# Every fourth gated row of the first placing round made on ScalarE instead of VectorE

## What is computed

```python
def _peer(h, wq, subkeys, u, v):
    q = (hf @ wq).reshape(n, PEER_HEADS, 2, PEER_QUERY_DIM // 2)
    s = jnp.einsum('nhpd,hpkd->nhpk', q, subkeys).astype(jnp.float32)
    sv, si = lax.top_k(s, PEER_TOPK)
    cand = (sv[:, :, 0, :, None] + sv[:, :, 1, None, :]).reshape(n, PEER_HEADS, PEER_TOPK * PEER_TOPK)
    cand_idx = (si[:, :, 0, :, None] * PEER_N_KEYS + si[:, :, 1, None, :]).reshape(n, PEER_HEADS, PEER_TOPK * PEER_TOPK)
    top_v, top_pos = lax.top_k(cand, PEER_TOPK)
    experts = jnp.take_along_axis(cand_idx, top_pos, axis=-1)
    gates = jax.nn.softmax(top_v, axis=-1).astype(h.dtype)
...
        act = jax.nn.gelu(jnp.einsum('td,tkd->tk', xb, u[eb]), approximate=False)
        return jnp.einsum('tk,tkd->td', gb * act, v[eb])
```

## Time and profile before

| what | value |
|---|---|
| median of 3 runs | 3841.91 us (3835.98 to 3842.95) |
| the profiled execution | 3840.35 us, span 3838.6 us |
| TensorE matmul busy | 3649.0 us (95%) |
| VectorE busy | 2594.1 us (68%) |
| GpSimd busy | 1618.4 us (42%) |
| ScalarE busy | 695.1 us (18%) |

### The profile page before, as it was taken

How to read it: one execution, slowest core, us unless ns; L and a number is a source line. 1 busy time by engine, 2 the same in 40 slices (tenths; PEclk the granted TensorE clock), 3 DMA queues, 4 the chain that set the end, 5 groups by cost and what they waited for, 6 DMA issues and landing times. The chain is left out here.

```text
span 3838.6 us, 39934 instructions
## 1 busy us (share of the span) xinstructions
PE 3649.0 (95%) x13726; PEld 2080.8 (54%) x13726; DVE 2594.1 (68%) x5994; ACT 695.1 (18%) x1579; POOL 1618.4 (42%) x1498
## 2 busy tenths in 40 slices
PE   5888899999999999999989898999999999999997
PEld 3455676555555555554455567765555555555543
DVE  7784999957666667676624749987776565565444
ACT  1242366200000000000013525661000000000000
POOL 0200255456566544454402005454777564444330
PEclk9999999999999999999999999999999999999999
DMA  7323145789999999999830122557999999899774
GB/s 271 108 79 121 39 132 154 265 332 391 380 373 374 376 378 373 379 372 359 354 125 2 63 110 78 158 154 280 409 410 410 379 349 365 341 358 361 286 298 156
DMA packets 365049, 1026.96 MB, mean 268 GB/s; under 512 B 30352, under 2 KB 132016, under 8 KB 364208
## 3 DMA queue, kind: packets, MB, share of 16 engines
q0 software_dynamic: 147456, 536.94, 36.5%
q1 hardware_dynamic: 118352, 436.07, 29.7%
q10 hardware_dynamic: 99040, 51.40, 4.8%
HBM read 965.07 MB, written 59.22 MB: 267 GB/s over the span
## 5 line engine op out<-in xcount | busy, mean ns | idle before, releaser
L1881 PE MATMUL ps<-colsT,arena 128*128 128x384 f32 x4096 | 1361.6, 487 | 7.0 <-DMA arena<-in_peer_ut 4.8
L1881 PEld LDWEIGHTS ps<-colsT,arena 128*128 128x128 f32 x4096 | 776.3, 190 | 588.2 <-issue 100.2
L1915 PE MATMUL ps<-arena 128*128 128x512 f32 x1536 | 676.5, 592 | 0.0
L1390 POOL DMA_INDIRECT proj<-in_peer_u,eidx x336 | 475.8, 1416 | 230.8 <-DVE modbc L1582 113.4
L1390 POOL DMA_INDIRECT proj<-in_peer_v,eidx x335 | 360.3, 1075 | 315.7 <-DVE colsT L1593 216.5
L1915 PEld LDWEIGHTS ps<-arena 128*128 128x128 f32 x1536 | 291.8, 190 | 345.2 <-issue 317.6
L1582 DVE CUSTOM_DVE_ANT_0 proj<-proj,rows 128x1024 f32<-128x1024 f32 x336 | 399.4, 1223 | 57.4 <-DMA proj<-in_peer_u,eidx 55.7
L1376 POOL TENSOR_SCALAR x<-iota,modbc 128x128 f32<-128x128 f32 x192 | 144.7, 770 | 680.9 <-ACT modbc L1710 554.9
L1593 DVE SCALAR_TENSOR_TENSOR colsT<-proj,modbc,colsT 128x1024 f32<-128x1024 f32 x330 | 409.7, 1286 | 12.6 <-DMA proj<-in_peer_v,eidx 12.5
L1915 PE MATMUL ps<-arena,x 128*128 128x512 f32 x768 | 337.7, 592 | 0.0
L1915 PE MATMUL ps<-arena,rows 128*128 128x512 f32 x768 | 337.7, 592 | 0.0
(11 more groups left out here) (294 smaller groups left out, 3719.1 us busy)
## 6 DMA issues: line engine op xcount, KB each, us to landing
arena<-in_peer_ut SPq DMA_DIRECT2D x256, 512.0 KB, 6.8
arena<-in_peer_v SPq DMA_DIRECT2D x256, 512.0 KB, 6.7
gmat_d<-arena ACTq DMA_DIRECT2D x24, 2048.0 KB, 9.3
arena<-gmat_d SPq DMA_DIRECT2D x64, 768.0 KB, 9.0
proj<-in_w_adaT SPq DMA_DIRECT2D x51, 512.0 KB, 9.1
modbc<-in_w_adaT SPq DMA_DIRECT2D x19, 512.0 KB, 8.9
rows<-in_w_adaT SPq DMA_DIRECT2D x18, 512.0 KB, 3.5
arena<-in_w_in SPq DMA_DIRECT2D x2, 4224.0 KB, 16.4
```

The source lines that it names most:

```text
L1390: pool.indirect_dma_start(ring[slots[at]], None, tab, bass.IndirectOffsetOnAxis(ap=eidx[:, b * SLOTS + q:b * SLOTS + q + 1], axis=0)).then ...
L1881: mm = pe.matmul(ps[:, 2 + j % 2, 0:ND], utab[:, j % UR, k], hT[:, k, NG:T], start=(k == 0), stop=(k == KT - 1))
L1915: mm = pe.matmul(ps[:, Y_BANKS[2 * d + c2], :], wT[j % CR][:, d * P:(d + 1) * P], vtab[:, j % VR, c2 * 512:(c2 + 1) * 512], start=(j == 0) ...
```

## The change

In round one (groups below 32 of each layer) VectorE leaves out the fourth token of each group, and ScalarE makes that row in two instructions: |j - column| by Abs with scale -1 and the index as bias, then Relu with the negated gate as scale and the gate as bias, which is the gate at distance zero and at most zero, so clipped, elsewhere. The negated gates come from one more copy in `turned_out` (region `ngT`). ScalarE makes these rows for the first four groups in one batch after the first marks, and later two at a time after the marks of a pair. TensorE waits for a new semaphore, `b_act`, besides `b_made`, whose count now goes by three a group in round one (`dve_rows`). Rounds two and three are untouched.

```diff
+        ngT = region(modbc, 2 * D + 7 * P, P)
...
+        def act_row(n):
+            return n < P // 4
...
+                        if t % 4 == 3 and act_row(n // 4):
+                            continue
                         dve.tensor_scalar(bring[:, n % B_TOK], iota128[:, :], ijgT[:, d % 2, 1, t:t + 1],
...
-                    c.link(act.activation(ijgT[:, d % 2, 0], ps[:, 0, 0:P], ACT.Copy, scale=-1.0))
+                    c.done(act.activation(ijgT[:, d % 2, 0], ps[:, 0, 0:P], ACT.Copy, scale=-1.0))
+                    if d == 0:
+                        c.done(act.activation(ngT, ps[:, 0, 2 * P:3 * P], ACT.Copy, scale=-1.0))
+                    c.wait()
...
+                def gated_rows(groups):
+                    groups = [n for n in groups if act_row(n)]
+                    if not groups:
+                        return
+                    if groups[0] < A_GRP:
+                        act.wait_ge(tr_out, 1)
+                    else:
+                        act.wait_ge(g_mm, groups[-1] - A_GRP + 1)
+                    for n in groups:
+                        t = 4 * n + 3
+                        c.done(act.activation(bring[:, t % B_TOK], iota128[:, :], ACT.Abs, scale=-1.0, bias=ijgT[:, 0, 1, t:t + 1]))
+                    c.wait()
+                    for n in groups:
+                        t = 4 * n + 3
+                        act.activation(bring[:, t % B_TOK], bring[:, t % B_TOK], ACT.Relu, scale=ngT[:, t:t + 1],
+                                       bias=ijgT[:, 0, 2, t:t + 1]).then_inc(b_act, 1)
...
+                        if pair + A_GRP < P // 4:
+                            gated_rows([d * (P // 4) + pair + A_GRP + h for h in range(2)])
...
                     for q in range(A_GRP):
                         mark_rows((k - 1) * (P // 4) + q)
+                    gated_rows([(k - 1) * (P // 4) + q for q in range(A_GRP)])
...
-                        pe.wait_ge(b_made, 4 * n + 4)
+                        pe.wait_ge(b_made, dve_rows(n))
+                        if act_row(n):
+                            pe.wait_ge(b_act, n + 1)
```

More of the change, by code:

```diff
@@ L198, in build @@
     sc_half = sem("sc_half")
+    b_act = sem("b_act")
     dots_ready, gelu_ready, coef_ready = sem("dots_ready"), sem("gelu_ready"), sem("coef_ready")
@@ L1274, in act_marks, with dve_rows @@
             return n % 2 == 0
+        def act_row(n):
+            return n < P // 4
+        def dve_rows(n):
+            return 4 * (n + 1) - min(n + 1, P // 4)
         def sc_row(r):
@@ L1706, in turned_out @@
                     if d >= 2:
-                        act.wait_ge(b_made, (d - 1) * P)
+                        act.wait_ge(b_made, dve_rows((d - 1) * (P // 4) - 1))
                         act.wait_ge(p_made, (d - 1) * (P // 2))
-                    c.link(act.activation(ijgT[:, d % 2, 0], ps[:, 0, 0:P], ACT.Copy, scale=-1.0))
+                    c.done(act.activation(ijgT[:, d % 2, 0], ps[:, 0, 0:P], ACT.Copy, scale=-1.0))
+                    if d == 0:
+                        c.done(act.activation(ngT, ps[:, 0, 2 * P:3 * P], ACT.Copy, scale=-1.0))
+                    c.wait()
                     act.activation(ijgT[:, d % 2, 1:3].rearrange("p a t -> p (a t)"), ps[:, 0, P:3 * P], ACT.Copy).then_inc(tr_out, 1)
```

## The result

| | before | changed |
|---|---|---|
| median | 3839.36 us (4 runs, 3835.98 to 3842.95) | 3864.21 us (4 runs, 3852.84 to 3865.75) |
| ratio, 95% interval | | 1.0058, 1.0047 to 1.007 |
| the profiled execution | 3840.35 us | 3852.84 us |

The kernel became slower by some 25 us, where 14.6 were forecast. 3864.21 lies inside the range of 3843 to 3866, but near its upper end and just above the 3848 to 3864 that were named for the mechanism alone. The profiled execution is the fastest of the four and only 12.5 us slower than the profiled one of before. The other three took 3863 to 3866; none of them was profiled, but the first experiment has the profile of another execution of this kernel that took as long.

What follows compares the result with a forecast made beforehand. VectorE ends round one, but ScalarE has no slack in steps without a query. Round two opens 7.3 us late in each layer; 14.6 us on the profiled 3840.35, plus 1.56 to the median, gives 3856.5 us, range 3843 to 3866.

Steps and rivals of the forecast that it cites:

- the mechanism: Round one: ScalarE's in-order new rows delay evictions TensorE waits for, where no query covers them; 7.3 us a layer, chance 0.57.
- Start: Opening of round one: an extra copy and the first gated rows on ScalarE make group 0 2.8 us late.
- Steps 0 and 1: Early round one: gated rows ahead of evictions on ScalarE make the following query 5.6 us late so far.
- Steps 2 and 3: A 7.3 us query on TensorE ahead of each hides two pairs' 2.84 us on ScalarE, with 0.8 to spare.
- To the end of step 5: Steps 3 to 5 add waits before groups 18 and 22; total lateness 9.7 us when step 5 ends.
- A pair: ScalarE's Abs and Relu work for two groups' gated rows: 1.42 us, bounds 0.98 and 1.76.
- The signals: Timeline signs: 8.5 us idle before group 0, VectorE waiting some 8 us, 0.6 before round two, 87.8 to its transposes.
- about 4 us of waiting before group 18: Sign in round one: TensorE waits about 4 us in front of group 18, for ScalarE's lines.
- The end of the round: Steps 6 and 7: VectorE's last rows end at 521.7, then 17.3 us; round two opens 7.3 us late.
- I let them cancel: TensorE's clock: 1.6 us a layer may return before round two, or be lost after step 5; range widened 3 us.
- slower still: Rival: the clock falls in steps 3 to 5 and nothing returns at round's end; 17.8 us, 3860, chance 0.21.
- the slow query behind the transposes: Filler opening round two: after 2.96 us of idling, clock 0.80, it took 8.7 instead of 7.1 us.

Runs made afterwards that it cites:

- the first experiment: The changed kernel run again with no edit: 3859.02 us (5 runs, 3852.13 to 3866.16), 1.0054 against the kernel before.
- ScalarE's work alone: Against the changed kernel, ScalarE makes its rows into a spare place and VectorE still makes all 128: 3863.74 us, 1.0067 against the kernel before.

## Why the prediction was right, and where its sizes were off

**The mechanism held, term by term.** Start: +2.8 forecast, 2.71 measured in the table, 2.82 in the kernel with the first four groups alone. Steps 0 and 1: +5.6 forecast, 5.80. Steps 2 and 3 hidden behind queries: the kernel with rows beside queries alone loses nothing there. To the end of step 5: +9.7 forecast, 10.11 measured from the transposes. A pair costs 1.50 instead of 1.42; for the six pairs behind the first four rows that is 0.5, about the difference. (The range counts six pairs with the first four rows among them as two; the working has eight, two for these rows, two in steps 0 and 1 and four in steps 3 to 5, so the bounds that follow from the price of a pair are somewhat too narrow.) ScalarE's work alone makes the whole loss. The rule of the Trainium skill (Perfetto Trace Analysis, Optimizing Scalar/DVE Operations) that moving work to ScalarE may make sense where VectorE is saturated held in this kernel for the 16 groups beside queries (0.9979) and not for all 32 (1.0058).

**The signals.** Group 0 idled 8.49 us (8.5 named), VectorE waited 9.9 us for TensorE (8 or more named), and from group 0 to round two's transposes it took 89.5, not 87.8. The wait before round two fell to 1.92, not to 0.6. One signal was mis-stated: I had named about 4 us of waiting before group 18; by my own terms it should have been 2.49 + 2.84 = 5.3, and it was 5.76.

**The end of the round, a wait missed.** What VectorE has to do behind its last gated rows went into the sum as 17.3 us, taken over from before. It holds the exponentials, which ScalarE then made in time. Now VectorE is ready for them 0.8 us before the last query's eviction begins (537.97 and 538.78), and they stand behind that eviction: VectorE's wait grew from 0.4 to 1.7, 1.3 us a layer. Putting them first took the same 1.3 off TensorE's wait. With 0.3 from step 5 that is the difference between 539.0 and 540.66.

**The clock, set to cancel.** "I let them cancel" is the step that failed. Nothing came back at the end of the round in the profiled execution (8.76 us at 0.80, as before), and the new waits cost either nothing or 4.5 us in a round. Both at their low: 12.5 us, as profiled. Both rounds in the long form: 9 us more, 21.5, where the medians of the first runs lie 24.9 apart and those of the second 21.3. That is the rival "slower still" in kind, though I priced it at 1.6 a layer and looked for it only after step 5; 2.84 of the 4.5 fall on group 6 and the query after step 1. So the mechanism gave the 14.6, but the median lies inside the range by what I had added to its upper end, and that was partly luck.

**What a shorter wait gives back.** The prediction tied the slow query behind the transposes to the 2.96 us of idling before it. After 0.61 and 0.62 us it took 7.07 in all four rounds that had such a wait (exponentials first, with all rows and with rows beside queries). But the length of the wait does not decide alone: after 1.92 it took 8.76 in the changed kernel and 7.07 with rows beside queries, and after 2.96 and 2.95 it took 8.76 and 7.07 in the two layers of one execution (the first four groups alone).

**One for one.** The prediction took it that what an earlier stage loses arrives at the end one for one. The profiles of before and after show 5.5 us less behind round one, which hide the 1.3 and 0.4 above, so that the short form came out close to the 14.6, but by errors that cancel. As the kernel with only the exponentials moved has 4.2 of the 5.5, this is for the most part a difference between executions; whether the change itself wins back any of the rest is not shown.

**What stays open.** What decides which form a round takes. The program is the same, the first waits nearly so, and one execution had both, so it is not the order of instructions alone. That the forms explain the runs between 3852 and 3866 is argued from two profiles of the changed kernel, not shown for each run, and the 4.4 us that the slowest profile has outside these rounds have no cause yet. Nor is it settled why the query that opens round two runs at one clock or the other.

## What to carry to other kernels

An engine's idle total says little: ask, step by step, what stands behind the moved work in that engine's order and who waits for it. Work for an idle in-order engine is free where its consumer has something long to do (here beside the queries: some 10 us gained, of which round one itself holds 4.6) and can cost its whole price elsewhere. When the moved work makes one engine earlier, look at every small result that it needs from the engine that became busier, here one row of exponentials and one square. And before a difference between two profiles is put down to a change, look for it in a third kernel that should not have it: here most of what seemed to come back behind round one was there too.

## What the hardware did that I had not expected

The same instructions with nearly the same waits (8.49, about 1.7 to 2.0, 1.8 to 3.3 us) ran in one execution, over 7 us from group 6 on, at a granted clock of 1.00 in layer 0 and 0.57 in layer 1, and the difference was 4.5 us in a stretch of 100. Filling three of the waits with products brought the early steps to full speed in both layers, but the clock was low again after later waits, so the round gained nothing over its short form. Five runs of the changed kernel lay 14 us apart (3852.13 to 3866.16), where 21 of the kernel before beside them stayed within 8.1 (3834.50 to 3842.61); in other sets the kernel before spread over 10 us (3837.14 to 3847.19), so its times are not steady either.
